# One wide and one narrow matmul in turn inside each Strassen half product, and one wait in place of two

## The chip, the cores and the metric

The kernel runs on one core of a Trainium2 chip. The metric is the device time of one execution in microseconds (us), lower is better. Before the change it is 2669.94 us, the median of 3 runs (2667.97 to 2670.22).

## The reference

One layer of a hybrid decoder trunk in float32, for 512 tokens of width 2048:

```
n = rms_norm(h, g_mix);  z = n @ w_in           # q | k | v | conv B, C, h | gate_attn | gate_conv
y_attn = sliding_window_sink_attention(rope(q), rope(k), v, sinks) @ w_attn_o
y_conv = gated_short_conv(ch, cb, cc, conv_w) @ w_conv_o
h = h + (sigmoid(ga) * y_attn + sigmoid(gc) * y_conv) @ w_out
h = h + memory_cross_attention(rms_norm(h, g_xattn), rms_norm(mem, g_mem), w_xq, w_xkv, w_xo)
gu = rms_norm(h, g_ffn) @ w_gate_up             # two halves of D_FF = 5632 columns
h = h + (silu(g) * u) @ w_down
out = rms_norm(h, g_final)
```

## The kernel before, in words

All activations lie transposed in SBUF, with channels on the 128 partitions and the 512 tokens along the free dimension. Every float32 factor is split in two fp32r parts, a rounded one (hi) and the rest (lo). An ordinary product of a 128x128 weight tile with 512 tokens is then three matmuls: hi x hi, hi x lo and lo x hi. The helper `columns` (L671 to L685) issues them as lines L679, L680 and L681, each over 512 columns, and waits once per weight block of 12 matmuls.

Two stages multiply by Strassen's scheme (in its form with seven products) instead: the gates of the mixer, `mix`, with 16 blocks, and most of the gate and up projection, `ffn`, with 40 blocks. Each block has seven products, P1, Q5, P2, P6, P7, P4 and P3, in the order that `cycle_products` (L105) gives. A product contracts 1024 channels for 256 tokens. It is made of two half products of four channel tiles each, so a stage has 14 half products per block: 224 in `mix` and 560 in `ffn`, 784 in all.

The moving operand of a half product is `both`, 256 columns of hi beside 256 columns of lo. For each of the four channel tiles `product` (L840) issues one wide matmul (L899, 512 columns: weight hi times `both`) and one narrow one (L903, 256 columns: weight lo times the hi half), which adds into the right half `r[:, 1, :]` of the same PSUM bank. Every matmul has its own load of 128x128 weights.

The weights come in slots. There are 8 slots for half products, each with a hi and a lo tile of 128x512. For each half product ScalarE writes hi (`block_hi`, L1239, semaphore `st.hi`, named block_weights_hi_ready) from the raw weights in `braw`, then VectorE subtracts (`block_lo`, L1835, semaphore `st.lo`, named block_weights_lo_ready). TensorE's last narrow matmul of a half product increments `st.used`, which frees the slot: ScalarE waits for it before it writes the half product eight places later, and it and VectorE wait for it before they read a product's PSUM bank. P6, P7, P4 and P3 add onto a bank that holds an earlier product, and wait until ScalarE has copied it out (L1257 `snap_b`, L1266 `snap_c`) or VectorE has read it. VectorE also forms the sums of the raw weights (L1843, L1850, L1856, L1862) and joins the results (L1874 to L1905).

The order on each engine is written out by hand, and each engine runs its instructions in that order. TensorE issues a half product as: wait for hi, four wide matmuls, wait for lo, four narrow matmuls.

Of the kernel before, what the change touches and what calls it, by code (L numbers as in the profile page):

```python
# [170 lines left out]
def build(nc, x, mem, g_mix, w_in, conv_w, sinks, w_attn_o, w_conv_o, w_out, g_xattn, g_mem,  # L171
          w_xq, w_xkv, w_xo, g_ffn, w_gate_up, w_down, g_final, rope, out):
    with ExitStack() as ctx:
# [103 lines left out]
        def operand(st, name, kp):  # L277

            if name in ("P1", "P2", "P4"):
                kt, t2 = 2 * kp + (name != "P1"), int(name == "P4")  # L280
                if st is mix:
                    return u_pair[:, kt, t2, :, :].rearrange("p a n -> p (a n)"), u_pair[:, kt, t2, 0, :]
                return h_both[:, t2, kt, :], h_both[:, t2, kt, 0:TH]
            both = st.sums[{"Q5": 0, "P6": 1, "P7": 2, "P3": 3}[name]]
            return both[:, kp, :, :].rearrange("p a n -> p (a n)"), both[:, kp, 0, :]
# [380 lines left out]
        def _(pe):  # L666
# [173 lines left out]
            def product(st, name, b):  # L840

                first, last = 4 * (st.last_group - 1), 4 * st.last_group
                if name == "P1":
                    r = st.reg_a[b % 2]
                    if b == 0:
                        pe.wait_ge(s_freed, first + 1)
                        if st is mix:
                            pe.wait_ge(s_ulo, KT)
                    elif b == 1:
                        pe.wait_ge(s_freed, first + 4)  # L850
                    else:
                        pe.wait_ge(st.g2, st.base + b - 1)
                elif name == "Q5":
                    r = st.reg_c[b % 2]
                    if b == 0:
                        pe.wait_ge(s_freed, first + 2)
                        if st is mix:
                            pe.wait_ge(s_mslo, 8)
                        else:
                            pe.wait_ge(s_slo, 16)  # L860
                    elif b == 1:
                        pe.wait_ge(s_freed, last + 1)
                    else:
                        pe.wait_ge(st.u1, st.base + b - 1)
                elif name == "P2":
                    r = st.reg_b[b % 2]
                    if b == 0:
                        pe.wait_ge(s_freed, first + 3)
                    elif b == 1:
                        pe.wait_ge(s_freed, last + 2)  # L870
                    else:
                        pe.wait_ge(st.g1, st.base + b - 1)
                elif name == "P6":
                    r = st.reg_a[b % 2]
                    pe.wait_ge(st.ca, st.base + b + 1)
                elif name == "P7":
                    r = st.reg_a[b % 2]
                    pe.wait_ge(st.cb, st.base + b + 1)
                    if st is mix and b == 0:
                        pe.wait_ge(s_mslo, 12)  # L880
                elif name == "P4":
                    r = st.reg_a[b % 2]
                    pe.wait_ge(st.cc, st.base + b + 1)
                else:
                    r = st.reg_c[b % 2]
                    pe.wait_ge(st.u2, st.base + b + 1)
                    if st is mix and b == 0:
                        pe.wait_ge(s_mslo, 16)
                if st is ffn and b == 0 and name == "P2":
                    pe.wait_ge(s_pl, KT)  # L890
                n, on = st.number(name, b), name in ("P6", "P7", "P4", "P3")
                for half in range(2):
                    if st is ffn and b == 0 and name == "P1":
                        pe.wait_ge(s_pl, (KP - 1, KT - 1)[half])
                    w_h, w_l = st.slot_hi[st.slot(n + half)], st.slot_lo[st.slot(n + half)]
                    pe.wait_ge(st.hi, n + half + 1)
                    for q in range(4):
                        both, _ = operand(st, name, 4 * half + q)
                        pe.matmul(r, w_h[:, q, :], both, start=(not on and half == 0 and q == 0), stop=False, skip_group_check=on)  # L899
                    pe.wait_ge(st.lo, n + half + 1)  # L900
                    for q in range(4):
                        _, u_h = operand(st, name, 4 * half + q)
                        mm = pe.matmul(r[:, 1, :], w_l[:, q, :], u_h, start=False, stop=(half == 1 and q == 3), skip_group_check=on)  # L903
                    mm.then_inc(st.used, 1)

            def products(st):

                product(st, "P1", 0)
                product(st, "Q5", 0)
                for b in range(st.blocks):  # L910
                    for name, n in cycle_products(b, st.blocks):
                        product(st, name, n)
# [79 lines left out]
            for h in range(XH):  # L992
# [3 lines left out]
                for c in range(MT):  # L996
                    mm = pe.matmul(B[h][:, :], vx[:, c, h * XHD:(h + 1) * XHD], pt_x[:, h, c, :],  # L997
                                   start=(c == 0), stop=(c == MT - 1))
# [1358 lines left out]
```

## Time and profile before

| | |
|---|---|
| median of 3 runs | 2669.94 us (2667.97 to 2670.22) |
| profiled execution, its own time | 2668.73 us |
| its span, first to last instruction | 2666.9 us |
| mean granted TensorE clock | 0.998 |
| busy, share of the span | PE 99%, weight loads 84%, VectorE 69%, ScalarE 45% |
| chain that ended last | PE 97%, VectorE 2% |
| of which L899 and L903 | 27% and 14% |

A busy share of PE counts a matmul from its start to its modelled end, and these overlap. What a matmul costs in a stream is therefore read from the distance between starts (called the pitch here), or from the number of matmuls in a stretch without idle time.

### The profile page before, as it was taken

To read this page: it belongs to the slowest core of one execution; us is meant where nothing else is said; L and a number is where in the kernel's file an instruction comes from. 1 tells how busy PE (TensorE), PEld (TensorE's weight loads), DVE (VectorE), ACT (ScalarE), POOL (GpSimd) and SP (SyncE) were. 2 spreads that over 40 slices of the span, in tenths; PEclk is the share of its full clock that TensorE was granted. 3 is DMA by queue.
4 is the path that set the end of the run, shared out by engine and by line. 5 is a ranking of instruction groups with operands and counts; after the bars stand their busy time and mean duration, and the time that the engine had idled before them with its cause. 6 is when DMAs were issued, how large, how long until landed. Compare 5 with 4: busy or idle time off the path is not lost.

```text
span 2666.9 us, 35423 instructions
## 1 busy us (share of the span) xinstructions
PE 2643.2 (99%) x13449; PEld 2248.9 (84%) x13449; DVE 1840.8 (69%) x3119; ACT 1208.7 (45%) x2263; POOL 56.0 (2%) x106
## 2 busy tenths in 40 slices
PE   8999999999999999999999999999999999999998
PEld 7888888888888888888888888888888888888887
DVE  3557776655999964457889999999999973234334
ACT  4334553434555543345655555555545542223221
POOL 0000000000000000000000000000000000000000
PEclk9999999999999999999999999999999999999999
DMA  5332222545445473333444343443434464344232
GB/s 167 95 89 84 74 80 80 193 146 160 144 139 165 131 258 118 100 105 117 152 116 133 115 134 108 122 128 115 131 111 119 131 217 130 124 139 129 95 96 93
DMA packets 329755, 338.97 MB, mean 127 GB/s; under 512 B 11292, under 2 KB 240756, under 8 KB 327028
## 3 DMA queue, kind: packets, MB, share of 16 engines
q1 hardware_dynamic: 318580, 288.48, 35.8%
q0 software_dynamic: 11008, 48.24, 4.6%
q8 instruction: 107, 1.75, 0.3%
q14 instruction: 60, 0.49, 0.1%
HBM read 299.98 MB, written 36.70 MB: 126 GB/s over the span
## 4 chain that ended last, share of the span: by engine, by line
PE 97%; DVE 2%; ACT 0%; issue 0%; DMA 0%; DVEq 0%; ACTq 0%
PE bank L899 27%; PE bank L679 16%; PE bank L680 16%; PE bank L681 16%; PE bank L903 14%; PE bank L694 2%; PE bank L696 2%; PE bank L695 2%; PE bank L801 1%; PE bank L787 0%; DVE y_out L2332 0%; PE bank L997 0%; PE bank L969 0%; DVE h_both L1604 0%; PE bank L775 0%
## 5 line engine op out<-in xcount | busy, mean ns | idle before, releaser
L1579 DVE TENSOR_TENSOR w_lo<-raw,w_hi 128x512 fp32r<-128x512 f32 x352 | 243.7, 692 | 477.0 <-ACT w_hi L1076 476.1
L1076 ACT ACTIVATE w_hi<-raw 128x512 fp32r<-128x512 f32 x352 | 222.3, 632 | 583.5 <-PE bank L681 580.8
L679 PE MATMUL bank<-h_both,w_hi 128*128 128x512 f32 x864 | 340.8, 394 | 0.0
L681 PE MATMUL bank<-h_both,w_lo 128*128 128x512 f32 x864 | 336.7, 390 | 0.0
L680 PE MATMUL bank<-h_both,w_hi 128*128 128x512 f32 x864 | 336.7, 390 | 0.0
L1581 DVE SCALAR_TENSOR_TENSOR w_lo<-raw,par,w_hi 128x512 fp32r<-128x512 f32 x192 | 143.7, 750 | 177.6 <-ACT w_hi L1076 176.7
L1835 DVE TENSOR_TENSOR w_lo<-braw,w_hi 128x512 fp32r<-128x512 f32 x392 | 251.4, 685 | 9.0 <-ACT w_hi L1239 9.0
L1239 ACT ACTIVATE w_hi<-braw 128x512 fp32r<-128x512 f32 x392 | 223.5, 626 | 39.5 <-PE bank L903 16.3
L1076 ACT ACTIVATE w_hi<-raw,par 128x512 fp32r<-128x512 f32 x192 | 138.5, 724 | 222.8 <-PE bank L681 136.2
L681 PEld LDWEIGHTS bank<-h_both,w_lo 128*128 128x128 f32 x864 | 162.2, 188 | 34.6
L679 PEld LDWEIGHTS bank<-h_both,w_hi 128*128 128x128 f32 x864 | 162.4, 188 | 31.5 <-issue 0.2
L680 PEld LDWEIGHTS bank<-h_both,w_hi 128*128 128x128 f32 x864 | 162.5, 188 | 31.3
L1835 DVE TENSOR_TENSOR h_both<-braw,h_both 128x512 fp32r<-128x512 f32 x280 | 179.3, 685 | 0.0
L899 PE MATMUL bank<-s_both,w_hi 128*128 128x512 f32 x640 | 174.8, 394 | 1.3 <-ACT snap_b L1257 1.3
L899 PE MATMUL bank<-s_both,h_both 128*128 128x512 f32 x640 | 174.7, 394 | 0.0
L1239 ACT ACTIVATE h_both<-braw 128x512 fp32r<-128x512 f32 x280 | 159.5, 626 | 14.2 <-PE bank L903 14.0
L679 PE MATMUL bank<-s_res,w_hi 128*128 128x512 f32 x416 | 161.8, 389 | 0.0
L680 PE MATMUL bank<-s_res,w_hi 128*128 128x512 f32 x416 | 161.8, 389 | 0.0
L681 PE MATMUL bank<-s_res,w_lo 128*128 128x512 f32 x416 | 161.8, 389 | 0.0
L1257 ACT ACTIVATE snap_b<-bank 128x512 f32<-128x512 f32 x56 | 33.5, 599 | 264.2 <-PE bank L903 264.2
L899 PE MATMUL bank<-h_both 128*128 128x512 f32 x480 | 131.1, 395 | 0.7 <-ACT snap_c L1266 0.7
L899 PE MATMUL bank<-h_both,w_hi 128*128 128x512 f32 x480 | 131.0, 394 | 0.0
(285 smaller groups left out, 5469.6 us busy)
## 6 DMA issues: line engine op xcount, KB each, us to landing
braw<-in_w_gate_up_dram SPq DMA_DIRECT2D x160, 512.0 KB, 4.8
raw<-in_w_down_dram SPq DMA_DIRECT2D x88, 512.0 KB, 3.7
raw<-in_w_in_dram SPq DMA_DIRECT2D x72, 512.0 KB, 3.7
braw<-in_w_in_dram SPq DMA_DIRECT2D x64, 512.0 KB, 4.9
raw<-in_w_out_dram SPq DMA_DIRECT2D x32, 512.0 KB, 3.7
hidden_spilled<-up_t POOLq DMA_DIRECT2D x44, 256.0 KB, 5.7
raw<-in_w_attn_o_dram SPq DMA_DIRECT2D x16, 512.0 KB, 3.8
raw<-in_w_conv_o_dram SPq DMA_DIRECT2D x16, 512.0 KB, 3.7
```

The lines of the kernel that those rows point to most:

```text
L679: pe.matmul(o_, w_hi[:, s, c], hi, start=(k == 0), stop=False)
L680: pe.matmul(o_, w_hi[:, s, c], lo, start=False, stop=False)
L681: mm = pe.matmul(o_, w_lo[:, s, c], hi, start=False, stop=(k == n - 1))
L694: pe.matmul(bk[j][:, :], hi[:, c], w_hi[:, s, :], start=(k == 0), stop=False)
L695: pe.matmul(bk[j][:, :], hi[:, c], w_lo[:, s, :], start=False, stop=False)
L899: pe.matmul(r, w_h[:, q, :], both, start=(not on and half == 0 and q == 0), stop=False, skip_group_check=on)
L903: mm = pe.matmul(r[:, 1, :], w_l[:, q, :], u_h, start=False, stop=(half == 1 and q == 3), skip_group_check=on)
L1076: nc.scalar.activation(w_hi[:, s, :], raw[:, n % RAW, (b0 + k) % 2, :], ACT.Copy, scale=sc).then_inc(s_hi, 1)
L1239: nc.scalar.activation(st.slot_hi[s], weights(name, b)[:, 4 * half:4 * half + 4, :], ACT.Copy).then_inc(st.hi, 1)
L1579: nc.vector.tensor_tensor(w_lo[:, s, :], src, w_hi[:, s, :], ALU.subtract).then_inc(s_lo, 1)
L1581: nc.vector.scalar_tensor_tensor(w_lo[:, s, :], src, g[:, k:k + 1], w_hi[:, s, :], ALU.mult, ALU.subtract).then_inc(s_lo, 1)
L1835: nc.vector.tensor_tensor(st.slot_lo[s], weights(name, b)[:, 4 * half:4 * half + 4, :], st.slot_hi[s], ALU.subtract).then_inc(st.lo, 1)
```

## The change

The four wide and four narrow matmuls of a half product are issued in turn, wide and narrow for each channel tile. The wait for `st.hi` is dropped; the wait for `st.lo`, which VectorE increments after it has read hi, stands ahead of the first matmul. The number of matmuls, their operands, the place of the increment of `st.used` and all other engines' programs are the same.

```diff
                     w_h, w_l = st.slot_hi[st.slot(n + half)], st.slot_lo[st.slot(n + half)]
-                    pe.wait_ge(st.hi, n + half + 1)
-                    for q in range(4):
-                        both, _ = operand(st, name, 4 * half + q)
-                        pe.matmul(r, w_h[:, q, :], both, start=(not on and half == 0 and q == 0), stop=False, skip_group_check=on)
                     pe.wait_ge(st.lo, n + half + 1)
                     for q in range(4):
-                        _, u_h = operand(st, name, 4 * half + q)
+                        both, u_h = operand(st, name, 4 * half + q)
+                        pe.matmul(r, w_h[:, q, :], both, start=(not on and half == 0 and q == 0), stop=False, skip_group_check=on)
                         mm = pe.matmul(r[:, 1, :], w_l[:, q, :], u_h, start=False, stop=(half == 1 and q == 3), skip_group_check=on)
                     mm.then_inc(st.used, 1)
```

TensorE before, one product in the middle of `ffn`, two half products (L899 are the wide matmuls, L903 the narrow ones; "waits" names the semaphores):

```order
L899 MATMUL bank<-s_both,h_both 128x512 [waits block_weights_hi_ready,p1_copied]
L899 MATMUL bank<-s_both,h_both 128x512 x3
L903 MATMUL bank<-s_both,h_both 128x256 [waits block_weights_lo_ready]
L903 MATMUL bank<-s_both,h_both 128x256 x3
L899 MATMUL bank<-s_both,h_both 128x512 [waits block_weights_hi_ready]
L899 MATMUL bank<-s_both,h_both 128x512 x3
L903 MATMUL bank<-s_both,h_both 128x256 [waits block_weights_lo_ready]
L903 MATMUL bank<-s_both,h_both 128x256 x3
```

TensorE after, one half product of the same stage and the start of the next (the narrow matmul is now L900):

```order
L899 MATMUL bank<-h_both 128x512 [waits block_weights_lo_ready]
L900 MATMUL bank<-h_both 128x256
L899 MATMUL bank<-h_both 128x512
L900 MATMUL bank<-h_both 128x256
L899 MATMUL bank<-h_both 128x512
L900 MATMUL bank<-h_both 128x256
L899 MATMUL bank<-h_both 128x512
L900 MATMUL bank<-h_both 128x256
L899 MATMUL bank<-s_both,w_hi 128x512 [waits block_weights_lo_ready,p1_p6_copied]
```

The width now changes after every matmul, in place of after every fourth, and the wait for lo has moved ahead of the wide matmuls.

## Rows read from the trace of the kernel before

**Rows 1.** The page: busy time by engine, and the chain by line.

```profile
PE 2643.2 (99%) x13449; PEld 2248.9 (84%) x13449; DVE 1840.8 (69%) x3119; ACT 1208.7 (45%) x2263; POOL 56.0 (2%) x106
...
PE bank L899 27%; PE bank L679 16%; PE bank L680 16%; PE bank L681 16%; PE bank L903 14%; PE bank L694 2%; PE bank L696 2%; PE bank L695 2%; PE bank L801 1%; PE bank L787 0%; DVE y_out L2332 0%; PE bank L997 0%; PE bank L969 0%; DVE h_both L1604 0%; PE bank L775 0%
```

**Rows 2.** Waits of TensorE, whole span: total us, times, longest.

```profile
PE bank L731 <- DMA x_nat<-in_x_dram: 5.9, 1, 5.9
PE bank L694 <- DVE w_lo L1581: 3.7, 1, 3.7
PE bank L710 <- DVE ssq L2033: 3.5, 1, 3.5
PE bank L899 <- ACT snap_b L1257: 2.3, 2, 1.3
PE bank L899 <- ACT snap_c L1266: 1.4, 2, 0.7
```

**Rows 3.** Stretches: ffn products, mixer products, an all-wide stretch: PE busy (matmuls), clock.

```profile
1430.00:2130.00 700.00, 700.00 (x3993) 1.00 0.41 122
680.00:940.00 260.00, 260.00 (x1485) 1.00 0.49 146
2210.00:2610.00 400.00, 400.00 (x1766) 1.00 0.37 118
```

**Rows 4.** Timeline, PE, inside ffn: start, us, engine, line, count.

```profile
1504.73 1.09 PE L899 MATMUL bank<-s_both,w_hi 128*128 128x512 f32 x4
1505.66 0.64 PE L903 MATMUL bank<-s_both,w_lo 128*128 128x256 f32 x4
1506.13 1.09 PE L899 MATMUL bank<-s_both,w_hi 128*128 128x512 f32 x4
1507.06 0.63 PE L903 MATMUL bank<-s_both,w_lo 128*128 128x256 f32 x4
1507.54 1.09 PE L899 MATMUL bank<-h_both 128*128 128x512 f32 x4
```

**Rows 5.** Timeline, PE, only wide matmuls (first and thirteenth of a stretch).

```profile
2299.81 0.39 PE L679 MATMUL bank<-s_res,w_hi 128*128 128x512 f32 x1
...
2302.53 0.39 PE L679 MATMUL bank<-s_res,w_hi 128*128 128x512 f32 x1
```

**Rows 6.** Timeline, PE, only narrow matmuls (first and thirty-seventh of a stretch).

```profile
1199.75 0.28 PE L680 MATMUL bank<-mem_t,w_hi 128*128 128x256 f32 x1
...
1204.07 0.28 PE L680 MATMUL bank<-mem_t,w_hi 128*128 128x256 f32 x1
```

**Rows 7.** Timeline, PE, six narrow matmuls between wide ones, attention stage.

```profile
230.10 0.39 PE L681 MATMUL bank<-h_both,w_lo 128*128 128x512 f32 x1
230.33 0.28 PE L801 MATMUL bank<-pt_hi,v_hi 128*128 128x256 f32 x1
230.44 0.28 PE L801 MATMUL bank<-pt_lo,v_hi 128*128 128x256 f32 x1
...
231.04 0.40 PE L679 MATMUL bank<-h_both,w_hi 128*128 128x512 f32 x1
231.28 0.40 PE L680 MATMUL bank<-h_both,w_hi 128*128 128x512 f32 x1
231.51 0.39 PE L681 MATMUL bank<-h_both,w_lo 128*128 128x512 f32 x1
...
233.79 0.28 PE L774 MATMUL bank<-k_hi,q_s 128*128 128x256 f32 x1
```

**Rows 8.** One line's instructions, L903: duration ns min/median/max.

```profile
L903 PEld LDWEIGHTS bank<-s_both,w_lo x640: 187/188/192, 1381.9 to 2160.4; 128*128 128x128 f32 x160
```

**Rows 9.** Timeline, a lo pair in ffn (VectorE) and the half products that use it.

```profile
1783.19 1.28 DVE L1835 TENSOR_TENSOR w_lo<-braw,w_hi 128x512 fp32r<-128x512 f32 x2
...
1785.39 1.09 PE L899 MATMUL bank<-s_both,w_hi 128*128 128x512 f32 x4
...
1786.80 1.09 PE L899 MATMUL bank<-s_both,w_hi 128*128 128x512 f32 x4
```

**Rows 10.** Timeline, last block of ffn: lo late, then the wait for snap_b.

```profile
2153.07 1.09 PE L899 MATMUL bank<-h_both,w_hi 128*128 128x512 f32 x4
2153.53 1.28 DVE L1835 TENSOR_TENSOR w_lo<-braw,w_hi 128x512 fp32r<-128x512 f32 x2
2154.27 0.74 PE L903 MATMUL bank<-h_both,w_lo 128*128 128x256 f32 x4
2154.85 1.08 PE L899 MATMUL bank<-h_both,w_hi 128*128 128x512 f32 x4
2155.76 0.63 PE L903 MATMUL bank<-h_both,w_lo 128*128 128x256 f32 x4
2157.73 0.97 PE L899 MATMUL bank<-s_both,w_hi 128*128 128x512 f32 x3 [1.34 <-ACT snap_b L1257]
```

**Rows 11.** The same place in the last block of the mixer.

```profile
946.64 1.29 DVE L1835 TENSOR_TENSOR u_pair<-braw,u_pair 128x512 fp32r<-128x512 f32 x2
946.90 1.09 PE L899 MATMUL bank<-u_pair 128*128 128x512 f32 x4
950.84 0.97 PE L899 MATMUL bank<-m_both,u_pair 128*128 128x512 f32 x3 [0.97 <-ACT snap_b L1257]
```

**Rows 12.** Stretch of ffn, all engines: PE, PEld, DVE, ACT, POOL busy.

```profile
1430.00:2130.00 700.00, 700.00 (x3993) 611.71 (x3992) 643.22 (x928) 368.60 (x682) 19.52 (x36) 1.00 0.41 122
```

## The prediction

> **What bounds the kernel now.** I read the page first, then the waits of TensorE, then stretches, then single starts. The page [rows 1] shows PE busy for 99% of the span, and a chain that ended last which runs over PE's own lines: L899 with 27% and L903 with 14%, some 1090 us, are the ones that the change reorders. The waits [rows 2] say that TensorE hardly ever waits for anyone: the two entries of L899 come to 3.7 us, and no entry of L903 is long enough to stand among the large ones. So the time of the two Strassen stages is the number of matmuls times the pitch between their starts, and the change can only act through that pitch, or by making a wait where there is none.
>
> The pitch is read in three places. In the product stages, 700.00 us hold 3993 matmuls and 260.00 us hold 1485 [rows 3]. With 8 matmuls per half product that is 700/499.1 = 1.4024 us and 260/185.6 = 1.4007 us, so 1.402 us per half product in the mean (560 of the one and 224 of the other). Single starts agree: 1504.73, 1506.13, 1507.54 [rows 4]; four wide ones take 0.93 us and four narrow ones 0.47. Where only wide matmuls follow one another, 12 pitches take 2302.53 - 2299.81 = 2.72 us, 0.2267 us each [rows 5], and 1766 of them fill 400 us [rows 3], the same. Where only narrow ones follow one another, 36 pitches take 1204.07 - 1199.75 = 4.32 us, 0.120 each [rows 6]. The granted clock is 1.00 in the product stages and in the all-wide stretch [rows 3], the level of 2.4 GHz, with PE busy throughout, so it explains no difference between them.
>
> Now the step on which everything rests. Four wide and four narrow matmuls at their undisturbed pitches would take 4 x (0.2267 + 0.120) = 1.3868 us. The half product takes 1.402. Some 0.0152 us per half product, 784 x 0.0152 = 11.9 us in the kernel, is the price of mixing the two widths as it is done now. The attention stage shows where it sits: after six narrow ones, which take 231.04 - 230.33 = 0.71 us where 6 x 0.120 = 0.72 were due, the 12 wide ones take 233.79 - 231.04 = 2.75 in place of 2.72, and the first two of them have pitches of 0.24 and 0.23 [rows 7]. So a run of narrow matmuls leaves something behind that the wide ones after it pay, 0.02 us on balance for one run. After a pause it is not there: the four wide ones behind the short stop at 2154.27 take 2155.76 - 2154.85 = 0.91 us, the undisturbed price, where those of the middle of the stage take 0.93 [rows 10, 4].
>
> **The change part by part.**
>
> *The matmuls and loads.* None is added or removed. Each matmul has its own load, all of the same 188 ns [rows 8], which is begun while the matmul ahead runs; four of eight loads lie beneath a narrow matmul before, and four of eight after. Nothing is gained or lost by the count.
>
> *The order.* Before, a half product has one run of four wide and one run of four narrow; after, four runs of one each. No place in the trace has one wide between two narrow ones, so the cost has to be bounded. Per pair, wide and narrow, the rows give: now 1.402/4 = 0.3505 us. Undisturbed 0.2267 + 0.120 = 0.3467. The lower end is a wide one at 0.2267 and a narrow one as short as the first of a run, 0.11 (230.33 to 230.44 [rows 7]; I take 0.113): 0.340 per pair, 1.360 per half product, 784 x (1.360 - 1.402) = -33 us. The upper end for a pair made of single pitches seen is a wide one right after a narrow one, 0.235 in the mean of the first two [rows 7], and a narrow one at 0.120: 0.355 per pair, 1.420, +14 us. I take 0.3467, which gives 1.3868 and -11.9 us. The reason is that the surcharge belongs to a run: what the wide ones pay was left by several narrow ones in a row, and it is gone as soon as TensorE has had slack. With the widths in turn no two narrow ones meet, and each has a wide one's 0.2267 us ahead of it. The estimate is nearest to the rows 5 and 6; it is not shown by them, since they hold no alternation.
>
> *The wait for hi that goes.* It costs nothing now: no wait for L1239 stands among PE's [rows 2]. Removing it gives 0.
>
> *The wait for lo that comes 0.93 us earlier.* In the steady stage lo is early enough. A close case in ffn is a P7: its two lo tiles are written by VectorE from 1783.19 to 1784.47, the first of them done by 1783.87, and the half products begin at 1785.39 and 1786.80 [rows 9], so 1.5 us and 2.3 us are left; the wait stays met. TensorE would gain only 0.015 us per half product on VectorE, which is busy 643.22 of 700 us there [rows 12] and stays below TensorE (92% would become 93%). Two places are late: in the last block of ffn the first lo is not written until about 2154.2, while the wide ones start at 2153.07 [rows 10]; in the last block of the mixer they start at 946.90, while the lo begun at 946.64 is ready at about 947.3 [rows 11]. The first would start 1.15 us later; 0.4 of that is already paid, since the narrow ones stop there now (the half product takes 2154.85 - 2153.07 = 1.78), so it shifts by 0.8 us, the second by 0.4. What is queued behind, the next half product and then P7, waits anyway for ScalarE's copy snap_b, 1.34 us and 0.97 us [rows 10, 11], and that copy stands behind sums and hi tiles made on VectorE and ScalarE, not behind these matmuls. So both delays end inside waits that exist: 0, with up to 1.2 us if the cover fails.
>
> *Slots and readers.* The increment of `st.used` stays on the last matmul, so slots and banks come free at the same step. 0.
>
> **The sum.** -11.9 + 0 = -12 us. Against the profiled execution's own time that is 2668.73 - 11.9 = 2656.8; the median of the runs stands 1.2 us above it, and the forecast for the median is 2669.94 - 11.9 = 2658.0 us. A measurement of this kernel can tell about 0.2%, 5.3 us, from no change; in the pair's terms that is 1.7 ns.
>
> **The rivals.**
>
> *The mix costs the same however it is grouped.* The surcharge would be a matter of the mean rate (8 loads and 8 matmuls in 1.4 us) and not of runs. For it: the wide pitch is raised during the whole run of four, and the kernel's 4 + 4 and the attention stage's 12 + 6 show surcharges of the same order. Against it: a stretch of narrow ones alone has the highest rate of all and shows an even 0.120 [rows 6]. Time: 2670 us. [...]
>
> *Every change of width is paid (the slower side).* The surcharge would belong to the step from narrow to wide. This happens once per half product now and four times after. The place is the first wide matmul behind a narrow one. For it: that first pitch is 0.24, not 0.227 [rows 7]. A mild form costs what single pitches show, 0.235 + 0.120, +14 us, 2684 us. In the full form each return to wide costs the whole 0.0152 us: 3 x 0.0152 x 784 = +36 us, 2706 us. Against the full form: the surcharge is spread over several wide ones, of which only the first would be left. It decides from a pair of 0.3505 us up; above 0.352 it is measurably slower.
>
> *The change does not reach the pitch because lo ends up late.* If VectorE, at 92%, were to fall behind by the 1.5 us of rows 9, each product would wait for it. TensorE's gain per block of 14 half products is only 0.2 us, and VectorE has 8% of slack; I give it next to nothing.
>
> *Better than the undisturbed sum*, with narrow ones at 0.113: 2637 us.
>
> **How the numbers follow.** Undisturbed pair: 0.45, with a range of its own from 2654 to 2664. Same cost in any grouping: 0.26. Each change paid, mild form: 0.17; full form: 0.07. Better than undisturbed: 0.04. Late lo: 0.01. Faster by over 0.2% is the first and the fifth, less a little of the first that may fall short, 0.47. Within 0.2% 0.27, slower 0.26. The range runs from 2650 to 2686: it takes in the likeliest case, no change and the mild form, and leaves out the full form, the gain of 33 us and the late lo, some 0.12, and a little more for the sizes.
>
> **What would show it.** Right: a stretch inside ffn with 8 matmuls per 1.387 us (some 4038 in 700 us in place of 3993), the same clock, wide starts 0.347 us apart, no new entry of L899 waiting for w_lo beyond the two last blocks. Wrong by the second rival: 1.40 us again, with other single pitches. Wrong by the third: pairs of 0.352 us or more. Wrong in the waits: entries of L899 behind L1835 in many blocks, each up to 0.9 us.

## The result, and the profile after

| | before | after |
|---|---|---|
| median (10 runs each) | 2669.78 us (2667.97 to 2670.22) | 2676.28 us (2674.61 to 2677.44) |
| ratio, 95% interval | | 1.0025 (1.0017 to 1.0033) |
| profiled execution, its own time | 2668.73 us | 2677.44 us |
| span, granted clock | 2666.9 us, 0.998 | 2675.7 us, 0.997 |

The kernel became 6.5 us slower, 0.25%, where 12 us less were forecast. The busy times of the other engines and the shares of the chain are those of before [rows 1]. The page of the kernel after, busy times and chain:

```profile
PE 2652.4 (99%) x13449; PEld 2249.8 (84%) x13449; DVE 1840.8 (69%) x3119; ACT 1206.9 (45%) x2263; POOL 55.7 (2%) x106
...
PE bank L899 27%; PE bank L679 16%; PE bank L681 16%; PE bank L680 16%; PE bank L900 14%; PE bank L694 2%; PE bank L696 2%; PE bank L695 2%; PE bank L801 1%; PE bank L787 0%; DVE y_out L2329 0%; PE bank L994 0%; PE bank L966 0%; DVE h_both L1601 0%; PE bank L775 0%
```

The stretches that answer to [rows 3], after (PE busy, number of matmuls, granted clock):

```profile
1430.00:2130.00 700.00, 700.00 (x3964) 1.00 0.41 120
680.00:940.00 260.00, 260.00 (x1474) 1.00 0.48 144
2210.00:2610.00 400.00, 400.00 (x1767) 1.00 0.37 120
```

In 700 us of `ffn` stand 3964 matmuls in place of 3993: 8 x 700/3964 = 1.4127 us per half product in place of 1.4024, and 1.411 in place of 1.401 in the mixer. Times 784 that is 8 us; the two profiled executions differ by 8.7 us, the medians by 6.5. In the all-wide stretch nothing moved (1767 against 1766), and the clock is the same. The timeline of PE, after, which answers to [rows 4]:

```profile
1504.70 0.40 PE L899 MATMUL bank<-s_both,h_both 128*128 128x512 f32 x1
1504.94 0.28 PE L900 MATMUL bank<-s_both,h_both 128*128 128x256 f32 x1
1505.05 0.40 PE L899 MATMUL bank<-s_both,h_both 128*128 128x512 f32 x1
1505.28 0.28 PE L900 MATMUL bank<-s_both,h_both 128*128 128x256 f32 x1
1505.40 0.40 PE L899 MATMUL bank<-s_both,h_both 128*128 128x512 f32 x1
1505.64 0.28 PE L900 MATMUL bank<-s_both,h_both 128*128 128x256 f32 x1
1505.76 0.40 PE L899 MATMUL bank<-s_both,h_both 128*128 128x512 f32 x1
```

Three pairs take 1505.76 - 1504.70 = 1.06 us, 0.3533 us each. They are not alike: the wide ones take 0.24, 0.23 and 0.24 us, the narrow ones 0.11, 0.12 and 0.12, and this rhythm of three pairs repeats through the stage. The waits of TensorE, after, with [rows 2]:

```profile
PE bank L899 <- ACT snap_c L1263: 1.4, 2, 0.7
PE bank L899 <- DVE w_lo L1832: 1.1, 1, 1.1
PE bank L899 <- ACT snap_b L1254: 0.7, 2, 0.4
...
PE bank L899 <- DVE u_pair L1832: 0.4, 1, 0.4
```

The early wait for lo makes TensorE stop only in the last block of each stage, for 1.1 and 0.4 us. The waits for snap_b fell from 2.3 us to 0.7. All waits of L899 together are 3.6 us, and were 3.7. So the time is in the pitch alone. One more thing shows only here, in the timeline of the last mixer block, after:

```profile
950.86 0.47 PE L899 MATMUL bank<-u_pair 128*128 128x512 f32 x1 [0.39 <-DVE u_pair L1832]
951.16 0.28 PE L900 MATMUL bank<-u_pair 128*128 128x256 f32 x1
951.28 0.40 PE L899 MATMUL bank<-u_pair 128*128 128x512 f32 x1
...
953.36 0.40 PE L899 MATMUL bank<-u_pair 128*128 128x512 f32 x1
```

Behind that stop six pairs take 953.36 - 951.28 = 2.08 us, 0.347 us each, not 0.353. The same order of the same matmuls has two prices.

### The profile page after: what moved, and what is told of

It reads as the page before. It is cut to its first block, busy times and chain, and to the rows that moved or that the text cites. A ratio compares the mean times of both kernels' runs of the same rounds, so it can differ in the third digit from the quotient of the medians.

```text
span 2675.7 us, 35423 instructions
## 1 busy us (share of the span) xinstructions
PE 2652.4 (99%) x13449; PEld 2249.8 (84%) x13449; DVE 1840.8 (69%) x3119; ACT 1206.9 (45%) x2263; POOL 55.7 (2%) x106
## 4 chain that ended last, share of the span: by engine, by line
PE 97%; DVE 2%; ACT 0%; issue 0%; DMA 0%; DVEq 0%; ACTq 0%
PE bank L899 27%; PE bank L679 16%; PE bank L681 16%; PE bank L680 16%; PE bank L900 14%; PE bank L694 2%; PE bank L696 2%; PE bank L695 2%; PE bank L801 1%; PE bank L787 0%; DVE y_out L2329 0%; PE bank L994 0%; PE bank L966 0%; DVE h_both L1601 0%; PE bank L775 0%
## 5 line engine op out<-in xcount | busy, mean ns | idle before, releaser
L679 PE MATMUL bank<-h_both,w_hi 128*128 128x512 f32 x864 | 340.8, 394 | 0.0
L680 PE MATMUL bank<-h_both,w_hi 128*128 128x512 f32 x864 | 336.7, 390 | 0.0
L899 PE MATMUL bank<-s_both,w_hi 128*128 128x512 f32 x640 | 229.4, 399 | 0.4 <-ACT snap_b L1254 0.4
L899 PE MATMUL bank<-s_both,h_both 128*128 128x512 f32 x640 | 229.3, 399 | 0.0
L900 PE MATMUL bank<-s_both,h_both 128*128 128x256 f32 x640 | 179.8, 281 | 0.0
L900 PE MATMUL bank<-s_both,w_lo 128*128 128x256 f32 x640 | 179.7, 281 | 0.0
L899 PE MATMUL bank<-h_both,w_hi 128*128 128x512 f32 x480 | 172.3, 399 | 1.1 <-DVE w_lo L1832 1.1
L899 PE MATMUL bank<-h_both 128*128 128x512 f32 x480 | 172.4, 399 | 0.7 <-ACT snap_c L1263 0.7
L679 PE MATMUL bank<-s_res,w_hi 128*128 128x512 f32 x416 | 161.9, 389 | 0.0
```

The costliest lines, as they stand in the source:

```text
L679: pe.matmul(o_, w_hi[:, s, c], hi, start=(k == 0), stop=False)
L680: pe.matmul(o_, w_hi[:, s, c], lo, start=False, stop=False)
```

## The experiments

Times are medians against the kernel before on the same chip (a single run where no interval is given, and a trace of one run each). "Per half product" is eight times the length of the stretch 1430 to 2130 us of the profile over its matmuls, unless another stretch is named; one matmul at its edge is 0.0004 us.

### Order or wait

`e1_lo_wait_only` keeps the order of before and takes the early wait; `e2_alternate_two_waits` takes the order and keeps both waits.

```diff
 # e1_lo_wait_only, against the kernel before
-                    pe.wait_ge(st.hi, n + half + 1)
+                    pe.wait_ge(st.lo, n + half + 1)
...
-                    pe.wait_ge(st.lo, n + half + 1)
 # e2_alternate_two_waits, against the change
-                    pe.wait_ge(st.lo, n + half + 1)
+                    pe.wait_ge(st.hi, n + half + 1)
...
+                        if q == 0:
+                            pe.wait_ge(st.lo, n + half + 1)
```

> Order of the kernel before (four wide, four narrow), with the one wait for lo ahead of the half product. Theory A (the order of the widths sets the pitch; the wait is free): the same time as before, within 1 us, 3993 matmuls in 700 us of ffn as before, and two waits of L899 for w_lo of 0.4 to 1.2 us in the last blocks that end inside the waits for snap_b. Theory W (the time of the change comes from the wait: a load that carries the wait for lo holds back the sequencer, or lo is late): slower by about what the change is, 6 to 7 us.

> Order of the change (wide, narrow in turn), with the two waits of the kernel before: hi ahead of the first wide, lo ahead of the first narrow. Theory A: as slow as the change, plus 6 to 7 us against before, 1.414 us per half product. Theory W: the time of before. If both order and wait carry a part, this and the run with the early wait alone add up to the change.

Measured: e1 2669.43 us against 2668.65, ratio 1.0002 (0.9993 to 1.0011), 1.403 us per half product. e2 2676.15 us, ratio 1.0025 (1.0015 to 1.0035), 3964 matmuls in 700 us, as in the change. So the order carries the whole difference and the wait, by itself, none that can be measured. Theory W has fallen, and with the change's 1.413 us theory B, the same cost in any grouping.

### The length of the runs

`e3_two_two` issues two wide, two narrow, twice. `e4_mirrored` turns the second half product of each product round, so that runs are eight long. `e8_runs_of_sixteen` turns every second product round.

```diff
 # e3_two_two, against the change
-                    for q in range(4):
-                        both, u_h = operand(st, name, 4 * half + q)
+                    for pair in ((0, 1), (2, 3)):
+                        for q in pair:
...
 # e4_mirrored: wide or narrow first, by half product
+                    for wide in ((True, False) if half == 0 else (False, True)):
...
 # e8_runs_of_sixteen: the same by product, over both half products
+                turned = n // 2 % 2 == 1
+                for step, (wide, half) in enumerate(((False, 0), (False, 1), (True, 0), (True, 1)) if turned else ((True, 0), (True, 1), (False, 0), (False, 1))):
```

> Two wide, two narrow, twice per half product, one wait for lo. Theory A in its form 'each return from narrow to wide is paid, less after a short run of narrow ones' (6.7 ns per return in the change's trace, 15 to 17 ns with runs of four, 20 ns with a long run): between 9 and 13 ns per return, 18 to 26 ns per half product over the undisturbed 1.387 us, so 1.405 to 1.413 us, and plus 2 to 7 us against before. Theory B (the surcharge goes with the mean rate, any grouping costs the same 15 ns): 1.402 us and the time of before; the change has already spoken against it.

> Half products mirrored: four wide, four narrow, then in the second half of a product four narrow, four wide, so that runs are eight long and there is one return from narrow to wide per product in place of two. Theory A: one return at about 20 ns per two half products, 10 ns each where before has 15 to 17, so 1.396 to 1.398 us per half product and 4 to 6 us less than before. Theory B: no change. Theory C (the surcharge is paid by each wide matmul behind a narrow run, whatever the number of returns, since it comes from a shortage that the run builds up): a run of eight leaves twice as much, no change.

> The order of whole products mirrored: eight wide, eight narrow in one product and eight narrow, eight wide in the next, so runs of sixteen and one return to wide per four half products. If each return after a long narrow run costs about 19 ns (four-four and the mirrored runs of eight show 17 and 19): 5 ns per half product, 1.391 us, about 9 us under the kernel before and 1 to 2 us under two-two. If the surcharge grows with the run of narrow ones: 1.396 us as with runs of eight. The wait for lo is needed earlier in every second product; if VectorE cannot follow, waits of L899's neighbours for w_lo appear and the time rises.

| run length | us | ratio to before (95%) | per half product | over 1.3867 | per return to wide |
|---|---|---|---|---|---|
| 1 (the change) | 2676.28 | 1.0025 (1.0017 to 1.0033) | 1.4127 | 26 ns | 6.5 ns |
| 2 (e3) | 2660.82 | 0.9971 (0.9960 to 0.9982) | 1.3927 | 6 ns | 3 ns |
| 4 (before) | | 1 | 1.4024 | 16 ns | 16 ns |
| 8 (e4) | 2662.51 | 0.9977 (0.9968 to 0.9986) | 1.3955 | 9 ns | 18 ns |
| 16 (e8) | 2658.62 | 0.9963 (0.9950 to 0.9977) | 1.3917 | 5 ns | 20 ns |

The last columns are worked out from the counts of the stretch; the undisturbed 1.3867 is from [rows 5, 6] (4 x (0.2267 + 0.120)). From runs of four up, the surcharge fits a fixed price of the return behind a narrow run, 16 to 20 ns, and longer runs save most of it. e4 and e8 came out nearly as expected, each a little better (6.1 us under the kernel before where 4 to 6 were expected, and 10.7 where 9 were), so theory C, in which a longer run leaves more, has fallen too. Two-two did not: 3 ns per return where 9 to 13 were expected, so it gains 7.8 us where a loss was expected. Runs of one and two do not lie on the line of the others, and not on one of their own. The stretches of PE, for e3 and then for e8:

```profile
1430.00:2130.00 700.00, 700.00 (x4021) 1.00 0.41 122
```

```profile
1430.00:2130.00 700.00, 700.00 (x4024) 1.00 0.42 122
```

The waits for snap_b and snap_c come to 4.2 us in e8 (3.7 before), and none is for w_lo, so VectorE kept up with the earlier need.

### Which property of the matmuls

Seven runs change the bank's half, the width or the loads. They compute something else than the reference asks (e6, e7 and e12 add into other columns of the sum, the runs with 64 weight columns leave out products for the output partitions 64 to 127), and only their pitch is read.

```diff
 # e6_alternate_left_half, against the change
-                        mm = pe.matmul(r[:, 1, :], w_l[:, q, :], u_h, ...
+                        mm = pe.matmul(r[:, 0, :], w_l[:, q, :], u_h, ...
 # e7_alternate_384 (in turn) and e12_four_four_384 (order of before)
+                        mm = pe.matmul(r.rearrange("p a n -> p (a n)")[:, P:4 * P], w_l[:, q, :], both[:, P:4 * P], ...
 # e5_alternate_64_columns (in turn), e11_four_four_64 (order of before); e9 the first line alone, save the first wide
 # matmul of each product; e10 the second alone, save the last narrow one of each product
+                        pe.matmul(r[0:64, :, :], w_h[:, q, 0:64], both, ...
+                        mm = pe.matmul(r[0:64, 1, :], w_l[:, q, 0:64], u_h, ...
```

> The order of the change, but the narrow matmul adds into the left half of the bank in place of the right one (the sum lands in the wrong columns; as much is computed). Theory P (the surcharge comes from adding to PSUM columns that the wide matmul ahead wrote shortly before): the distance to the same column becomes 227 ns in place of 120, and the pitch changes. Theories L and S: 1.413 us, no change.

Measured: 2677.54 us, 3965 matmuls in 700 us (3964 in the change). The half of the bank has no part in it; theory P has fallen.

> The order of the change, with 384 columns in the narrow matmul in place of 256 (128 columns more are added than the sum needs). Undisturbed, a pair would be 0.2267 + 0.1733 = 0.400 us and a half product 1.600. Theories L and S: a matmul that long covers its load and its instructions, no surcharge, 1.600 us. If the surcharge belongs to a change of length as such: 6.7 ns per pair stay, 1.627 us.

> Four wide and four of 384 columns (128 columns more than the sum needs), waits as before. In turn, the 384-column matmuls kept a surcharge of 6.7 ns per return (1.627 us where 1.600 is undisturbed). If a return from a run of four costs as much as with 256 columns: 1.617 us. If one change costs 6.7 ns whatever the run, once the narrower one is longer than its load: 1.607 us. If a run of matmuls longer than their loads leaves nothing behind: 1.600 us.

Measured, in turn: 2842.41 us and 3444 matmuls in 700 us, 1.626 us per half product, 6.5 ns per pair over the undisturbed 1.600. Four-four: 2837.15 us, 3459 matmuls, 1.619 us, 19 ns per return. The 1.600 is an estimate, since no stretch holds 384 columns alone; it takes 0.1733 us, halfway between rows 5 and 6, and in a run of four of e12 the pitch is 0.175 (four in 0.70 us):

```profile
1506.12 0.86 PE L903 MATMUL bank<-s_both,w_lo 128*128 128x384 f32 x4
1506.82 1.08 PE L899 MATMUL bank<-s_both,w_hi 128*128 128x512 f32 x4
```

So a narrow matmul that streams half as long again pays about the same surcharges. This speaks against theories L and S, which both expected 1.600. It does not settle whether a load that outlasts its matmul matters, since the load's record of 188 ns [rows 8] is still longer than 0.175 us. None of the three numbers for four-four that were expected fits exactly; the nearest is 1.617.

> The order of the change, with only 64 of the 128 weight columns loaded and computed in the half products (the output's partitions 64 to 127 get no product). The count of loads and matmuls and the streamed columns are those of the change. Theory L (the surcharge of 27 ns per half product over the undisturbed 1.387 us comes from the weight load that must fit beneath a narrow matmul): a load of half the size takes it away, 1.387 us or less per half product, 21 us or more under the change. Theory S (it comes from the supply of instructions, two per matmul, which is too slow beneath a narrow one): 1.413 us as in the change.

> The order of the change; the wide matmuls load and compute only 64 weight columns, save the first of each product, and the narrow ones stay whole. A wide matmul's load runs while the narrow one ahead streams. Theory L1 (what costs is the load that lies beneath a narrow matmul): at most 1.387 us per half product, down to the 1.360 us of the run with 64 columns everywhere. Theory L2 (what costs is the load that lies beneath the wide one, or the sum of both): 1.400 to 1.413 us.

> The order of the change; the narrow matmuls load and compute only 64 weight columns, save the last of each product, and the wide ones stay whole. Their load runs while the wide one ahead streams. Theory L1: the surcharge stays, 1.413 us. Theory L2: it falls to 1.387 us or less. If each load adds a part of its own wherever it lies, this and the run with narrow loads for the wide matmuls share the 53 ns between 1.413 and 1.360 us.

> The order and waits of the kernel before; all half-product matmuls load and compute 64 weight columns. It gives the undisturbed pitches with short loads inside runs. Theory L (all surcharges are of the loads): no surcharge for the return from narrow to wide, and the same 1.360 us per half product as in turn, so the order makes no difference with short loads. If the surcharge of a return has another cause: 10 to 20 ns more than 1.360 us.

| weight columns | us | per half product |
|---|---|---|
| in turn, 64 everywhere (e5) | 2635.39 | 1.360 |
| in turn, wide ones 64 (e9) | 2641.66 | 1.367 |
| in turn, narrow ones 64 (e10) | 2657.73 | 1.389 |
| four-four, 64 everywhere (e11) | 2645.16 | 1.3725 |

(e5 and e9 in the time in which PE is busy, 259.51 us with 1527 matmuls and 698.79 us with 4091.) The load's own record, L900 in e5, falls from 188 ns [rows 8] to 134:

```profile
L900 PEld LDWEIGHTS bank<-s_both,w_lo x640: 133/134/137, 1372.5 to 2128.3; 128*64 128x64 f32 x160
```

With short loads the pair in turn takes 0.340 us, below the 0.3467 that I called undisturbed, so theory S, which expected 1.413 us of e5, has fallen. How much of it is due to the shorter loads is less sure. Against the change e9 takes off 46 ns per half product and e10 23; against 1.387 us, at which the same order can run too (next section), e9 takes off 20 and e10 nothing. By either count it is the load of the wide matmul, which runs beneath a narrow one, whose shortening goes with more. But a matmul with 64 weight columns also writes only 64 partitions of the bank, and no run separates this from the shorter load. And with short loads four-four still pays 12 ns over in turn (e11 against e5), so shorter loads do not make the order free, and theory L in its plain form has fallen with e7 and e11. The Trainium skill ("TensorE: Matmul & The Clock Gate", section "Back-to-back issue gap") says that in a stream of loads and matmuls both set the spacing. These runs agree as far as they separate the two (1.360 us in e5, 1.387 at best with whole loads); its figure for 512 columns, about 131 ns, does not fit the 227 of [rows 5].

### Two rhythms

After these twelve runs it was open why in turn costs 0.3533 us when the trace of the change has stretches at 0.347. Four runs change nothing but what each stage begins with.

```diff
 # f1, f2, f3, against the change: groups of tiles, wide ones then narrow ones
+                    groups = ((0, 1), (2, 3)) if n % 14 == 0 and b == 0 and name == "P1" and half == 0 else ((0,), (1,), (2,), (3,))
+                    for group in groups:
...
 # f1 has ((0, 1, 2, 3),) there, f3 ((0, 1, 2), (3,))
 # f4_small_ahead, ahead of the first half product of a stage
+                        for _ in range(8):
+                            pe.matmul(r[:, 0, 0:64], w_h[:, 0, :], operand(st, name, 0)[0][:, 0:64], start=True, stop=True)
```

> The order of the change, save the first half product of each of the two stages, which runs four wide, four narrow. Theory R (in turn there are two steady rhythms, 0.3533 and 0.3467 us per pair, and what ran just before decides which): a stage may run at 1.387 us per half product to its end, 21 us less than the change for both stages, 15 us for ffn alone; it may as well fall into the dear rhythm. Theory O (the order costs 0.3533 us once the after-effect of a stop is used up): 1.413 us in both stages, the time of the change.

> The same with two wide, two narrow, twice, in the first half product of each stage. Theory R: 1.387 or 1.413 us per half product, by stage. Theory O: 1.413 us.

> The same with three wide, three narrow, one wide, one narrow in the first half product of each stage. Theory R: 1.387 or 1.413 us per half product, by stage. Theory O: 1.413 us.

> The order of the change with eight matmuls of 64 columns ahead of the first half product of each stage, into the bank that it clears next (they cost under 1 us per stage). Theory R: 1.387 or 1.413 us per half product, by stage. Theory O: 1.413 us, up to 2 us above the change.

Measured: f1 2674.59, f3 2675.07, f4 2679.28 us, with 1473, 1473 and 1474 matmuls in the mixer's 260 us and 3964 in the 700 us of `ffn`: all in the dear rhythm of the change. f4 is 3.0 us above the change, more than the 2 us expected at most. f2 2669.61 us. Its stretches:

```profile
680.00:940.00 260.00, 260.00 (x1503) 1.00 0.50 151
1430.00:2130.00 700.00, 700.00 (x3963) 1.00 0.41 121
```

In f2 the mixer holds 1503 matmuls, 0.346 to 0.347 us per pair, and this from its start to its last block, 300 us later. Two swaps of neighbouring matmuls at the start of the stage went with another price for the next 1700. `ffn` holds 3963, the dear rhythm. It began in the cheap one at 1374.02 and lost it 19 us into the stage, in PE's timeline of f2:

```profile
1393.43 0.40 PE L901 MATMUL bank<-h_both 128*128 128x512 f32 x1
1393.66 0.28 PE L904 MATMUL bank<-h_both 128*128 128x256 f32 x1
1393.78 0.40 PE L901 MATMUL bank<-h_both 128*128 128x512 f32 x1
1394.02 0.28 PE L904 MATMUL bank<-h_both 128*128 128x256 f32 x1
1394.14 0.40 PE L901 MATMUL bank<-h_both 128*128 128x512 f32 x1
1394.38 0.28 PE L904 MATMUL bank<-h_both 128*128 128x256 f32 x1
1394.49 0.40 PE L901 MATMUL bank<-h_both 128*128 128x512 f32 x1
1394.72 0.28 PE L904 MATMUL bank<-h_both 128*128 128x256 f32 x1
```

The pair at 1393.43 still takes 0.35 us; the three wide pitches from 1393.78 on are 0.24, 0.24 and 0.23, the dear pattern. The view of waits names none there. The place is the start of the fifteenth half product of the stage, and the loads (PEld) and VectorE's line for its lo, in the same timeline of f2, show that lo only just arrives:

```profile
1392.52 1.29 DVE L1836 TENSOR_TENSOR h_both<-braw,h_both 128x512 fp32r<-128x512 f32 x2
...
1393.09 0.39 PE L901 MATMUL bank<-s_both,h_both 128*128 128x512 f32 x1
1393.09 0.19 PEld L904 LDWEIGHTS bank<-s_both,h_both 128*128 128x128 f32 x1
1393.32 0.28 PE L904 MATMUL bank<-s_both,h_both 128*128 128x256 f32 x1
1393.33 0.19 PEld L901 LDWEIGHTS bank<-h_both 128*128 128x128 f32 x1
```

The first of the two lo tiles is done at 1393.21, 0.22 us before the half product starts, the shortest lead in `ffn` outside its last block. The load that carries the wait for it starts 9 ns behind the matmul ahead, where every other load of the product stages, outside the stops of the last blocks, starts 2 to 5 ns behind. So a delay of about 6 ns by the early wait for lo probably threw the stage into the dear rhythm. This is read from one trace; no run tests it, for instance by giving f2 the two waits of before.

So theory R holds and theory O has fallen: 224 half products at 0.0266 us less are 6.0 us, and the one run of f2 is 6.7 us under the median of the change.

The last two runs renew the two-two, per block and per product.

```diff
 # g1_two_two_per_block, g2_two_two_per_product
+                    groups = ((0, 1), (2, 3)) if name == "P1" and half == 0 else ((0,), (1,), (2,), (3,))
+                    groups = ((0, 1), (2, 3)) if half == 0 else ((0,), (1,), (2,), (3,))
```

> In turn, save the first half product of every block (P1), which runs two wide, two narrow, twice. If two-two leads into the cheap rhythm from either one: 1.387 us per half product in both stages, 0.0157 us less than before in each of 784, 12 us under the kernel before, about 2657 to 2658 us. If it does so only from a run of wide matmuls, as at the start of the mixer: the mixer is cheap and ffn may stay at 1.413 us, 2669 to 2670 us. If every two-two in the middle disturbs the rhythm: 1.41 us, 2676 us.

> In turn in the second half product of each product, two wide, two narrow, twice in the first. If two-two leads into the cheap rhythm from either one: between 1.387 us (in turn, cheap) and 1.393 us (two-two throughout) per half product, 9 to 12 us under the kernel before. If not: between 1.393 and 1.413 us, from 8 us under to 1 us over it.

Measured: g1 2655.97 us against 2668.21, ratio 0.9960 (0.9947 to 0.9972); g2 2659.18 us, ratio 0.9964 (0.9951 to 0.9977), 1.389 us per half product. The stretches of g1, and its timeline of PE inside `ffn`:

```profile
680.00:940.00 260.00, 260.00 (x1502) 1.00 0.51 151
1430.00:2130.00 700.00, 700.00 (x4039) 1.00 0.41 122
```

```profile
1801.21 0.39 PE L901 MATMUL bank<-s_both,w_hi 128*128 128x512 f32 x1
1801.44 0.27 PE L904 MATMUL bank<-s_both,w_lo 128*128 128x256 f32 x1
1801.56 0.40 PE L901 MATMUL bank<-h_both 128*128 128x512 f32 x1
...
1803.29 0.39 PE L901 MATMUL bank<-h_both 128*128 128x512 f32 x1
```

Six pairs take 1803.29 - 1801.21 = 2.08 us, 0.3467 each, and 4039 matmuls in 700 us make 1.3865 us per half product, in both stages. This is the best version of the study: 12 us under the kernel before, 20 us under the change, with one wait per half product. One of its 8 runs took 2669.85 us, the other seven 2655.15 to 2656.57. 14 us more are what `ffn` would cost in the dear rhythm (560 x 0.026), but no trace was taken of that run, so this stays a guess. In the traced run lo is again only 0.23 us ahead of two half products, so a late lo may have done it there as in f2; in that case the two-two of later blocks did not lead back from the dear rhythm.

## Why the prediction was wrong

*What bounds the kernel* held: the pitch of L899 and its partner carries the whole difference, at the same clock, with no time outside the product stages.

*The step that failed* is "I take 0.3467, which gives 1.3868 and -11.9 us", the price of the pair. The change's pair takes 0.3532 us (1.4127/4), 1.4127 us per half product, +8 us. The reason given for it, that the surcharge belongs to a run of narrow matmuls and that in turn there is none, holds for runs of four, eight and sixteen (16 to 20 ns per return), and was carried over to a run length of one for which no row spoke. In turn there are two steady rhythms, 0.3467 and 0.3533 us, and the change runs in the dear one from the start of each stage. The value was a real one: g1 reaches it and with it the forecast time, 2656.0 us, but the change does not.

*The bounds* (0.340 to 0.355) held the measured pair, and the range held the time; the range took in a gain, no change and a loss, so this says little for the mechanism. Of the rivals the one on the slower side came nearest by the price of the pair (0.355 against 0.3532; the same cost in any grouping was 0.3505), while by the time the 2676 us lie between its 2684 and the other's 2670, a little nearer to 2670. It did not come near by its mechanism. It said that every return to wide is paid. Two-two has two returns per half product and pays 3 ns each, and the cheap rhythm has four and pays nothing. Its sign was right because the wide pitch right behind a narrow one, 0.235 in [rows 7], is indeed what the change shows in the mean (1.4127 us less four narrow ones at 0.117 leave 0.236 for each wide one). That row was the only one about a wide matmul next to a narrow one, and I had put it at the end of the range. The rival of the same cost in any grouping has fallen: 1.387 to 1.413 us by grouping.

*The waits* held: dropping the wait for hi costs nothing, the wait for lo is met in the steady stage and its two stops end inside the waits for snap_b (3.6 us in all against 3.7), as e1 confirms with 1.0002. But the P7 of [rows 9], with lo 1.5 us ahead, was not the closest case of the stage. At the fifteenth half product lo is ahead of its start by 0.42 us in the kernel before, 0.57 us in the change and 0.22 us in f2, where the wait may have cost the rhythm, an effect that the prediction did not consider. *Slots and readers, the count of loads* held as far as the runs go.

Still open is what in the chip the rhythms are. The totals (three pairs in 1.06 us, the gain with 64 weight columns, about the same surcharge with a longer narrow matmul) bound it, but no run here names the resource.

## What to carry to other kernels

In this kernel, where TensorE hardly ever waits, the order of matmuls of different widths was worth some tenths of a per cent either way (0.40% less in g1, 0.25% more in the change): compare single starts of exactly the sequence that is to be used, and where the trace holds no such sequence, count its price as unknown in both directions. Grouping widths in long runs came out here nearly as expected and steadily (runs of sixteen gained 0.37%, five runs within 1.6 us). An alternation can be cheaper still, but look whether the pitch is the same from the start to the end of a stage, since a few instructions at its start, and perhaps one operand that arrives a few nanoseconds late, can set the price of all that follow.

## What was not expected of the hardware

The same alternating stream of wide and narrow matmuls ran at 0.3533 or 0.3467 us per pair for hundreds of microseconds, at a granted clock of 1.00 and without a wait, and in f2 and g1 two swaps of neighbouring matmuls at the start went with the cheaper one. In f2 the stream changed from one to the other at the one load that started 9 ns behind the matmul ahead, where the others start 2 to 5 ns behind. A weight load of 64 columns in place of 128 (134 against 188 ns in its record) took 26 ns off a half product below the undisturbed price, 1.360 against 1.387 us, though every load lies beneath a running matmul; such a matmul also writes half the partitions, which is not separated. Widening the narrow matmuls from 256 to 384 columns left both surcharges about as they were, 6.5 ns per pair in turn and 19 ns per return in four-four (16 with 256 columns).
